# Scaling and adding eight modulation blocks on GpSimd, and the dilated score products on both halves of the rows

## What is computed

```python
for l in range(DEPTH):                      # DEPTH = 1
    last = l == DEPTH - 1
    mod_x = jnp.split((jax.nn.silu(c) @ w_ada[l] + b_ada[l])[:, None, :], N_MOD, axis=-1)
    mod_c = jnp.split((jax.nn.silu(c_ctx) @ w_ada[l] + b_ada[l])[None, None, :], N_MOD, axis=-1)
...
    x = x + mod_x[2] * merge(o_x, g_x, hy_x)
    x = x + channel_mix(x, mod_x)           # uses mod_x[3], mod_x[4], mod_x[5]
```

```python
DIL_CONFIGS = ((128, 1), (512, 4), (2048, 16))
for g, (window, dilation) in enumerate(DIL_CONFIGS):
    sl = slice(g * DIL_HEADS, (g + 1) * DIL_HEADS)
    o, lse = dilated_window_attention(q[:, :, sl], k[:, :, sl], v[:, :, sl], window, dilation)
```

## Time and profile before

| what | value |
|---|---|
| median of three runs | 1556.63 us (1551.86 to 1559.81) |
| profiled execution, its own time | 1560.95 us |
| its span | 1559.2 us |
| PE, DVE, ACT busy | 1305.2, 481.3, 296.7 us |
| GpSimd busy | 0.2 us, 4 instructions |
| transfers | 492.24 MB, mean 316 GB/s |
| first mixer | to about 268 us of the span |
| experts of the first block | to about 696 us |
| second block, layer 0 | to about 1126 us |
| second block, layer 1 | to 1559 us |

### The profile page before, as it was taken

The page is one execution under the profiler, slowest core; times in us unless marked ns, Lnnn a source line. Parts: engine busy times, 40 slices in busy tenths (PEclk is TensorE's granted clock), DMA queues, the critical chain, the costliest instruction groups (busy, mean ns, idle before and its releaser), DMA issues.

```text
span 1559.2 us, 18728 instructions
## 1 busy us (share of the span) xinstructions
PE 1305.2 (84%) x7664; PEld 740.1 (47%) x7664; DVE 481.3 (31%) x1156; ACT 296.7 (19%) x616; POOL 0.2 (0%) x4
## 2 busy tenths in 40 slices
PE   7999999966656656579999999856999999998558
PEld 4565787412212212157868743321577687443214
DVE  5125473101101101013774522110237745221102
ACT  2422211100000000022322312200223223122002
POOL 0000000000000000000000000000000000000000
PEclk9999999978888787799999999977999999999879
DMA  9475288999999999994521499999925214999995
GB/s 402 167 266 220 108 321 380 409 427 427 427 429 428 426 428 427 428 424 210 216 100 63 169 391 378 406 422 420 422 103 216 107 56 163 381 381 415 423 422 217
DMA packets 39534, 492.24 MB, mean 316 GB/s; under 512 B 4368, under 2 KB 4752, under 8 KB 6288
## 3 DMA queue, kind: packets, MB, share of 16 engines
q1 hardware_dynamic: 39296, 490.80, 76.4%
q10 hardware_dynamic: 144, 0.13, 0.0%
HBM read 489.86 MB, written 1.05 MB: 315 GB/s over the span
## 4 chain that ended last, share of the span: by engine, by line
PE 64%; DMA 29%; DVE 5%; issue 1%; ACT 0%; SPq 0%; DVEq 0%
PE PS L668 21%; DMA A<-ring_d 20%; DMA A<-ranked_d 9%; PE PS L1600 7%; PE PS L1033 4%; PE PS L1444 4%; PE PS L1583 4%; PE PS L1627 3%; PE PS L673 3%; PE PS L973 2%; PE PS L1565 2%; PE PS L1668 2%; PE PS L740 1%; PE PS L1654 1%; PE PS L1381 1%
## 5 line engine op out<-in xcount | busy, mean ns | idle before, releaser
L668 PE MATMUL PS<-A 128*128 128x256 f32 (+4 forms) x1552 | 365.4, 393 | 4.4 <-DVE A L2090 1.0
L1033 PE MATMUL PS<-A 128*32 128x512 f32 x1472 | 223.7, 746 | 132.8 <-DMA A<-ring_d 132.3
L668 PEld LDWEIGHTS PS<-A 128*128 128x128 f32 x1552 | 272.4, 193 | 89.4 <-issue 53.1
L1033 PEld LDWEIGHTS PS<-A 128*32 128x32 f32 x1472 | 50.3, 124 | 293.9 <-issue 233.3
L1600 PE MATMUL PS<-A 128*32 128x512 f32 (+1 forms) x768 | 116.9, 695 | 76.4 <-DMA A<-ranked_d 76.4
L1600 PEld LDWEIGHTS PS<-A 128*32 128x32 f32 (+1 forms) x768 | 33.1, 130 | 150.3 <-issue 150.3
L2155 DVE TENSOR_TENSOR A<-A,PS 128x512 f32<-128x512 f32 x8 | 5.5, 688 | 318.8 <-PE PS L1033 318.8
L2656 DVE TENSOR_TENSOR A<-A,PS 128x256 f32<-128x256 f32 x22 | 9.3, 422 | 234.1 <-ACT A L3211 234.1
L1627 PE MATMUL PS<-A 128*32 128x512 f32 (+1 forms) x512 | 80.2, 596 | 0.5 <-issue 0.5
L673 PEld LDWEIGHTS PS<-A 128*128 128x128 f32 (+1 forms) x396 | 45.4, 144 | 47.4 <-issue 27.3
L673 PE MATMUL PS<-A 128*128 128x128 f32 (+1 forms) x396 | 58.5, 279 | 10.8 <-DVE A L2155 7.1
(11 more groups left out here) (398 smaller groups left out, 1296.3 us busy)
## 6 DMA issues: line engine op xcount, KB each, us to landing
A<-ring_d SPq DMA_DIRECT2D x155, 2048.0 KB, 26.0
A<-ranked_d SPq DMA_DIRECT2D x48, 2048.0 KB, 11.4
A<-ranked_d SPq DMA_DIRECT2D x48, 1024.0 KB, 19.7
A<-ring_d SPq DMA_DIRECT2D x2, 1312.0 KB, 28.6
A<-ring_d SPq DMA_DIRECT2D x2, 1280.0 KB, 24.0
A<-xT_d SPq DMA_DIRECT2D x1, 1024.0 KB, 5.5
A<-cT_d SPq DMA_DIRECT2D x1, 1024.0 KB, 12.0
A<-pf_d SPq DMA_DIRECT2D x2, 512.0 KB, 19.3
```

The source lines that it names most:

```text
L668: ins = g.matmul(out, l, r, start=n == 0, stop=n == len(pairs) - 1)
L1033: ins = g.matmul(ps[32 * e:32 * e + 32, :], rows_of(kk, e), wv[4 * (kk % 2) + e], start=kk == 0, stop=kk == 7)
```

## The change

There are two parts. In the first, blocks 4 to 11 of `w_ada` go to GpSimd. For each block it multiplies the eight chunks by the activated vector `c`, one scalar for each partition, in place (8 `tensor_scalar` of 128x512; the first writes to `ACC`), and adds them up in `ACC` (7 `tensor_tensor` of 128x512). The scaling of the next chunk is issued ahead of the addition that waits for the one before. TensorE then only sums over the 128 partitions: `sums` 0 for blocks 4 to 7 and `sums` 1 for blocks 8 to 11, 4 matmuls each, whose stationary operand `PICK` is a column of ones among zeros. `ACC` lies in slot 11, so SP waits for `sums` 1 ahead of the first block of that slot. A ring slot that holds such a block is free when GpSimd has read it. Only `c`, not `c_ctx`, is multiplied with these blocks, so `mod` 1 has half the columns. In `AFTER`, `ada` 11 now stands behind `hy` 4. In the second part, the middle configuration of a dilated head lies in the other half of the rows (the host rolls its 128 weight columns by 64), and the six matmuls come in another order.

```diff
+         ("ada", 11): ("hy", 4), ("sums", 0): ("hy", 4), ("sums", 1): ("ic", 0, 1), ("mod", 1): ("ic", 0, 3), ("sp", 0): ("ada", 9), ("sp", 1): ("ada", 10)}
...
-LATE = [("ada", b) for b in range(4, 12)] + [("mod", 1)]
+LATE = [("ada", b) for b in range(4, 12)] + [("sums", 0), ("sums", 1), ("mod", 1)]
...
+        PICK = take(33)
+        ACC = V(COLS - SLOT, 8, 512)
...
-            r, hp = rows64(u % 2), u // 2
-            return [(QKC[r, 6 * hp + cfg, :], QKC[r, 6 * hp + 3 + cfg, :], r,
+            hp, mine = u // 2, [rows64((u + cfg) % 2) for cfg in (0, 1, 0)]
+            return [(QKC[mine[cfg], 6 * hp + cfg, :], QKC[mine[cfg], 6 * hp + 3 + cfg, :], rows64(u % 2),
...
             def ada(blk):
                 w, i = weights("ada", blk)
+                if blk > 3:
+                    return
...
+            def sums(h):
+                if h == 0:
+                    fresh("ada", 1, hold=True)
+                    g.wait_ge(*at("pick"))
+                g.wait_ge(*at("acc", 4 * h + 7))
+                for q in range(4):
+                    ins = g.matmul(bank("ada", 1)[32 * q:32 * q + 32, :], PICK[:, 1 - h:33 - h], ACC[:, 4 * h + q, :], start=h == 0, stop=h == 1,
+                                   skip_group_check=True)
+                ins.then_inc(*(full("ada", 1) if h else up("pe")))
...
-                for x, (q, k, *_) in enumerate(heads):
-                    g.matmul(ps[:, x, 0:128], q[:, 0:128], k[:, 0:128], start=True, stop=True)
-                for x, (q, k, *_) in enumerate(heads):
-                    ins = g.matmul(ps[:, x, 128:384], q[:, 128:256], k, start=True, stop=True)
+                for x, ti in ((0, 0), (1, 0), (2, 0), (1, 1), (0, 1), (2, 1)) if n == 3 else ((0, 0), (1, 0), (0, 1), (1, 1)):
+                    q, k = heads[x][0:2]
+                    c = slice(128 * ti, 128 * ti + 128 * (ti + 1))
+                    ins = g.matmul(ps[:, x, c], q[:, ti * 128:(ti + 1) * 128], k[:, 0:128 * (ti + 1)], start=True, stop=True)
...
+        def pool(p):
+            p.wait_ge(*at("scp"))
+            for blk in range(4, 12):
+                i = order.index((("ada", blk), SLOT))
+                w, acc = RING[SLOTS[i]].rearrange("p (k n) -> p k n", k=8), ACC[:, blk - 4, :]
+                p.wait_ge(*at("landed", i))
+                p.tensor_scalar(acc, w[:, 0, :], SCP[:, 0, 14:15], None, ALU.mult).then_inc(*up("pool"))
+                p.tensor_scalar(w[:, 1, :], w[:, 1, :], SCP[:, 1, 14:15], None, ALU.mult).then_inc(*up("pool"))
+                for k in range(1, 8):
+                    ready = now("pool")
+                    if k < 7:
+                        p.tensor_scalar(w[:, k + 1, :], w[:, k + 1, :], SCP[:, k + 1, 14:15], None, ALU.mult).then_inc(*up("pool"))
+                    p.wait_ge(*ready)
+                    p.tensor_tensor(acc, acc, w[:, k, :], ALU.add).then_inc(*(up("pool", "acc", blk) if k == 7 else up("pool")))
+                note("pool", "read", i)
...
+                if i == SLOTS.index(LAST_SLOT):
+                    q.wait_ge(*at("full", "ada", 1))
```

More of the change, by code:

```diff
@@ L727, in ada @@
             def ada(blk):
-                n = int(blk > 3)
-                first, last = ((0, 3), (4, 11))[n]
                 w, i = weights("ada", blk)
+                if blk > 3:
+                    return
                 wv = w.rearrange("p (k n) -> p k n", k=8)
-                if blk == first:
-                    fresh("ada", n, hold=True)
-                c = 14 - 2 * (blk - first)
+                if blk == 0:
+                    fresh("ada", 0, hold=True)
+                c = 14 - 2 * blk
                 g.wait_ge(*at("scp"))
@@ L739, in ada @@
                     for q in range(4):
-                        ins = g.matmul(bank("ada", n)[32 * q:32 * q + 32, :], SCP[:, 2 * q + kk, c:c + 32], wv[:, 2 * q + kk, :],
-                                       start=blk == first and kk == 0, stop=blk == last and kk == 1, skip_group_check=True)
-                ins.then_inc(*(full("ada", n) if blk == last else up("pe")))
+                        ins = g.matmul(bank("ada", 0)[32 * q:32 * q + 32, :], SCP[:, 2 * q + kk, c:c + 32], wv[:, 2 * q + kk, :],
+                                       start=blk == 0 and kk == 0, stop=blk == 3 and kk == 1, skip_group_check=True)
+                ins.then_inc(*(full("ada", 0) if blk == 3 else up("pe")))
                 finished(i)
-                if blk == last:
-                    banks.release("ada", n)
+                if blk == 3:
+                    banks.release("ada", 0)
+            def sums(h):
[7 more added lines that the diff above has]
+                ins.then_inc(*(full("ada", 1) if h else up("pe")))
+                if h:
+                    banks.release("ada", 1)
             def mod(n):
-                w = (8, 16)[n]
                 ps = fresh("mod", n)
@@ L999, in tensor @@
             sig.stage = "mix"
-            steps = dict(w1=w1, w2=w2, ht=ht, sp=sp, ada=ada, mod=mod, xsum=xsum, csum=csum, hy=hy, ut=ut, cv=cv, ic=ic,
+            steps = dict(w1=w1, w2=w2, ht=ht, sp=sp, ada=ada, sums=sums, mod=mod, xsum=xsum, csum=csum, hy=hy, ut=ut, cv=cv, ic=ic,
                          q=q, k=k, v=v, g=gate, a=a_, gates=gates, b=b, kt=kt, st=st, scr=scr, o=o_, osum=osum, ob=ob, wr=wr, out=out_, rows=rows)
@@ L1794, in vector @@
             v.memset(SCP, 0.0).then_inc(*out("scp0"))
+            v.memset(PICK, 0.0).then_inc(*out())
+            settle()
+            v.memset(PICK[:, 1:2], 1.0).then_inc(*out("pick"))
             def w1():
@@ L2807, in ada, with sums, row @@
             def ada(blk):
-                if blk not in (3, 11):
-                    return
-                n = int(blk > 3)
+                if blk == 3:
+                    row(0)
+            def sums(h):
+                if h:
+                    row(1)
+            def row(n):
                 full("ada", n)
@@ L3393, in overflow_sync @@
                 q.wait_ge(*at("full", "xd", l, 31, 7))
-        for engine in (tensor, vector, scalar, sync):
+        for engine in (tensor, vector, scalar, pool, sync):
             engine(Counted())
@@ L3415, in _ @@
             scalar(s)
+        @block.gpsimd
+        def _(p):
+            sig.start()
+            pool(p)
         @block.sync
```

22 lines of the change are left out of this document (13 added, 9 removed).

## The result

The changed kernel takes 1611.71 us (1611.53 to 1613.24, four runs), the kernel before beside it 1557.97 us (1551.86 to 1559.81, four runs). The ratio is 1.0349, interval 1.0331 to 1.0366: slower by 53.7 us. The forecast was 1546.0 us with a range to 1562. The profiled execution takes 1611.53 us, its span is 1609.7 us.

The account below looks back on a forecast made before the run. TensorE was taken to bound the first mixer, weight transfers the first block's experts. Part one's 7.2 us plus part two's 4.4 less 1 for contention gave 10.6 us off 1556.6, so 1546.0 us; range 1539 to 1562.

Parts of the forecast that it names:

- P: GpSimd's time for one `ada` block in the first mixer, taken as 13.0 us; up to 12.1 us was to cost nothing.
- 76.3 + 5P: Time in us at which `("hy", 0)` lands in the first mixer, through the shared slot; 141.3 at P = 13.
- The price of "8": In the first mixer, each further us of P costs 8 us once `sums` 1 waits as well.
- the stream of weights: Transfers for the first block's experts, issued at 227.51 us; ending `ic` 1 earlier was to move them all.
- Rival C: Slower through the first mixer's slot chain, P over 15.2, GpSimd and DVE holding each other up; 1566 us, chance 0.17.
- The upper bound, the RECIPROCAL row: GpSimd at the rate of DVE's RECIPROCAL: 3.5 us an operation, P 52 us, costing some 200 us.
- If GpSimd were never late, `ic` 1 would end 11.8 us sooner: Part one's full gain in the first mixer: 13.7 us removed from TensorE, 1.86 us added for the sums.
- Blocks 4 to 8 and 11: Late `ada` blocks on TensorE in the first mixer; removing these six was to save 6 x 1.86 = 11.2 us.
- Block 10: The `ada` block ahead of `sp` 1; it and the 0.64 us wait for DVE both go, 2.5 us.
- Contention: DVE operations with two SBUF inputs against GpSimd, between `cv` 0 and `ic` 0: 1 us lost, ends 0 and 6.
- The clock: Granted in full (1.00) in the mixer's stretches from 66 us on, so no part was expected from it.
- Part two: Dilated score matmuls in the attention: 0.55 us less a unit, eight units, 4.4 us; ends 0 and 6.9.

Follow-up runs that it names:

- scale_bcast: Changed kernel with each GpSimd scaling written as a tensor_tensor with the scalar column broadcast along the row; 1582.29 us, ratio 1.0162 to the kernel before.
- no_scale: Changed kernel with all 64 GpSimd scalings left out, additions kept; 2753.72 us because the branch for overfull experts ran, so only its mixer is read, 155.71 us.
- no_fill: Kernel before with part two, GpSimd idle, blocks 9, 10 and 11 moved so nothing fills the waits at the two `sp`; 1557.19 us, ratio 0.999.
- gps_beside: dil_only with GpSimd also doing five blocks' worth of such operations, scaling by a constant, on its own memory; 1550.86 us, ratio 0.9967 to the kernel before.
- dil_only: Kernel before with only the second part of the change, the modulation staying on TensorE; 1549.93 us against 1559.54, ratio 0.9945.
- gps_only: Changed kernel without its second part, the dilated products as before; 1620.07 us, ratio 1.0401 to the kernel before.

## Why the prediction was wrong

The step that failed first is P, "8 x 0.61 + 7 x 1.22 = 13.4 us". The additions were right (1.25), the scalings were sized from a DVE row and took 1.54. The arithmetic behind it held: `("hy", 0)` was to land at 76.3 + 5P, 141.3 us with P = 13, and it landed at 189.1. Of the 47.8 us between, 43.6 are P (the first five blocks took 108.6 us, not 65), 2.9 the longer way from issue to landing (31.2 us for four, not 28.3), and 1.3 the later start at 49.3. The price of "8" per us once `sums` 1 waits was measured as 7.4 (`scale_bcast`). One reading was wrong without harm: SP's longest wait in the mixer is not the 23.0 us of the earlier trace rows but 31.3 us, for an `ada` block. That the stream of weights starts behind `ic` 1 held all the same (the second block comes 62.7 us later, the output projection 60.6).

Rival C had the mechanism, the place (`("hy", 0)`, then `sums` 1) and the sign, and stopped at P = 16.7. With 21.6 its own rule gives 1566 + 8 x 4.9 = 1605 us against 1611.7 measured. Its reason, GpSimd and DVE holding each other up, was not the cause. In the first block DVE has no operation from 60 to 66 us, and the scalings take 1.54 all the same. The window of the kernel after, columns as in the earlier trace rows:

```profile
60.00:66.00 6.00, 6.00 (x19) 2.89 (x19) 0.00 (x0) 0.40 (x1) 6.00 (x5) 1.00 0.00 0
```

The upper bound, the RECIPROCAL row, would have held the truth and was dropped as "not believed"; between 9.2 and 52 the likeliest case was placed at the low end on DVE's rows alone. The trace agrees with the ratio for `tensor_tensor` in the Trainium skill, page "GPSIMD Engine Reference", section "Performance versus the Vector engine": 1.25 us is 1.8 to 2.0 times DVE's 0.68 to 0.61. The sum by it, P = 14.2, was wrong all the same, since it left the scaling at DVE's 0.61. The Trainium skill, same page, section "Engine selection", calls one-input work "roughly line-rate". Here that work, 1.54 us, is dearer than the two-input addition, and the measurement decides.

The second step that failed would have spoiled the forecast even with a fast GpSimd: "If GpSimd were never late, `ic` 1 would end 11.8 us sooner". `no_scale` gives 4.0. Three things are in the difference, and the clock is a fourth.

- "Blocks 4 to 8 and 11 stand among steps with which TensorE is never idle, so 6 x 1.86 = 11.2 us come off the path": not block 8. "That DVE work starts from the end of the step at 132.20" put the start of DVE's chain 7.5 us too late (133.2 instead of 125.74); it hangs on `g` 3, which stands ahead of block 8. So block 8 is hidden beside it as block 9 is: together they gave 0.5 us in the kernel after, where 1.9 was counted.
- Block 10 was priced at 2.5 us with its wait, but behind `sp` 1 comes `scr` 1, which needs DVE and waits 1.98 us after. So block 10 is worth about half a us at full clock; from `sp` 0 to `scr` 1 it is 10.8 us after and 9.8 before, since the two `sp` ran 1.6 us slower. This is the rule "where a stall goes, say what is late next", not followed to the next step.
- Contention, taken as 1 us with ends 0 and 6 at `cv` 0, took 2.7 us in `no_scale`, ahead of `sp` 0. In the kernel after GpSimd stood idle when DVE made these products, and it took nothing there.

The clock was to give no part. It cost some 2 us (1.6 in the kernel after), since TensorE now stood idle ahead of `sp`: here the window in `no_scale`.

```profile
133.50:138.00 4.50, 4.43 (x6) 1.90 (x7) 0.00 (x0) 0.58 (x1) 4.26 (x4) 0.51 0.93 331
```

Part two was right in mechanism and a little small in size: 0.66 us a unit instead of 0.55, 5.3 us in the attention instead of 4.4. The long instructions hide more behind each other than the 0.3 us allowed.

What stays open: where the 5 us of `no_fill` outside the mixer come from, what a DVE delay of 2.7 us would cost with the eight blocks on TensorE, and why a GpSimd scaling takes 1.54 us. That it is not DVE, and that the scalar from memory makes up at most 0.09 us of it, is shown; what it is was not tried.

## What to carry to other kernels

Before work is given to an engine that the trace has never shown at work, time one of its operations in the very form that will be used; a factor of 2.5 on one of two forms decided this change, because a chain of slots multiplied it by 5 to 8. Work taken off the busiest engine is worth only what the next engine's chain lets through: find where the chain of the engine that is waited for begins, and leave the steps between there and the wait where they are. A helper engine should be given as much as it does between two uses of its slot and no more: four blocks made the mixer 6.7 us shorter where eight made it 60 us longer.

## What the runs showed of the hardware

GpSimd on 128x512 fp32, from start to start, undisturbed: scaling by a scalar from memory 1.54 us, by a constant 1.45; product with a repeated column 1.00 (1.11 on average); sum of two tensors 1.25. With DVE on two SBUF tensors at the same time, single GpSimd scalings took 1.7 to 2.5 us in the kernel after and DVE's products 1.0 to 1.84 instead of 0.69. Not each was stretched: in `gps_beside` most kept 0.69 while GpSimd worked.

TensorE's clock fell behind some waits and not behind others. Behind waits of 2.46 and 2.50 us in `no_fill` it was granted in full (1.00 from 136 to 149 us). After 4.06 us of idleness in the kernel after it was 0.57 from 146 to 150 us, and 1.00 from 150 to 154.8; after 5.21 in `no_scale` it was 0.51, the lower level of 1.2 GHz. 0.57 is a stretch with both levels, 1.2 and 2.4, mostly the lower. A similar step lies in the router of the second block. Here the first layer in the kernel before, then in `dil_only`, window (columns as in the earlier trace rows) and the row of TensorE:

```profile
880.00:890.00 10.00, 9.20 (x33) 5.89 (x34) 5.74 (x28) 5.20 (x11) 0.00 (x0) 0.83 0.07 30
...
882.08 5.81 PE L668 MATMUL PS<-A 128*128 128x512 f32 x12 [0.49 <-DVE A L2468]
```

```profile
878.00:888.00 10.00, 9.47 (x42) 6.43 (x44) 7.26 (x34) 5.95 (x13) 0.00 (x0) 1.00 0.04 16
...
879.80 4.12 PE L668 MATMUL PS<-A 128*128 128x512 f32 x12 [0.49 <-DVE A L2468]
```

The same twelve instructions take 5.8 us in the first layer of both kernels without part two and 4.12 in all twelve with it. In the second layer both lengths occur with part two; of the two kernels without it, one has 5.81 and one 4.12. Whether part two causes the first was not tested. It would be 1.7 us of its gain, but between `gps_only` and the kernel after the second layer takes it back (4.12 against 5.80).
